# Attention with the values' projection last, and weight splits that wait for GpSimd's sum

## The reference, cut to what matters

```python
h = rmsnorm(x, norm_mix_2[i])          # x * rsqrt(mean(x*x) + eps) * gain
x = x + mixer(h)
x = x + (silu(rmsnorm(x, norm_ffn_2[i]) @ wg) * (rmsnorm(x, norm_ffn_2[i]) @ wu)) @ wd
```

```python
q, k, v = split(h @ w_qkv, [1024, 1280])
q, k = rmsnorm(q per head, q_gain), rmsnorm(k per head, k_gain)
logits = q @ k.T / 8 + bias, masked to a distance of at most 128
m = max(logits, sink); pr = exp(logits - m)
pr = pr / (sum(pr) + exp(sink - m))
out = (pr @ v) @ w_o
```

## Time and profile before

| | |
|---|---|
| median of 3 runs | 2970.85 us (2970.27 to 2976.11) |
| profiled execution | 2971.51 us, span 2969.6 us |
| mean granted clock of PE | 0.991 |
| PE busy | 2897.0 us, 98% |
| DVE, ACT, POOL busy | 2037.6, 1627.0, 330.4 us |
| DMA | 613.26 MB, mean 207 GB/s |
| attention, first projection to output projection | 2051.5 to 2147.1 us |

### The profile page before, as it was taken

The page is one execution under the profiler, slowest core; times in us unless marked ns, Lnnn a source line. Parts: engine busy times, 40 slices in busy tenths (PEclk is TensorE's granted clock), DMA queues, the critical chain, the costliest instruction groups (busy, mean ns, idle before and its releaser), DMA issues.

```text
span 2969.6 us, 46613 instructions
## 1 busy us (share of the span) xinstructions
PE 2897.0 (98%) x20144; PEld 2679.1 (90%) x20144; DVE 2037.6 (69%) x1842; ACT 1627.0 (55%) x1603; POOL 330.4 (11%) x224
## 2 busy tenths in 40 slices
PE   8999999999999999999999999999899999999999
PEld 8999999999988888888888787999799999896999
DVE  6787665678768888888888765555555555575553
ACT  6456544545657767767677552445654454362542
POOL 1130310113010000000000002101021111002210
PEclk9999999999999999999999999999999999999999
DMA  7444555544549989989899531556155545540453
GB/s 235 155 142 157 172 185 173 184 145 145 165 181 372 347 346 373 351 335 355 344 370 370 166 128 43 171 177 234 44 170 181 188 150 184 192 142 29 154 180 122
DMA packets 359730, 613.26 MB, mean 207 GB/s; under 512 B 11519, under 2 KB 323925, under 8 KB 324576
## 3 DMA queue, kind: packets, MB, share of 16 engines
q1 hardware_dynamic: 355936, 597.99, 57.8%
q10 hardware_dynamic: 3104, 12.10, 1.2%
q0 software_dynamic: 480, 0.12, 0.0%
HBM read 608.99 MB, written 1.05 MB: 205 GB/s over the span
## 4 chain that ended last, share of the span: by engine, by line
PE 94%; DVE 2%; ACT 2%; POOL 1%; issue 1%; DMA 0%; ACTq 0%; SPq 0%; POOLq 0%; DVEq 0%
PE ps L329 19%; PE ps L330 18%; PE ps L331 18%; PE ps L1269 5%; PE ps L1271 5%; PE ps L1270 5%; PE ps L1245 3%; PE ps L1247 3%; PE ps L1246 3%; PE ps L1810 2%; PE ps L689 2%; PE ps L1825 2%; PE ps L1319 1%; PE ps L1778 1%; PE ps L1766 1%; POOL work L392 1%
## 5 line engine op out<-in xcount | busy, mean ns | idle before, releaser
L273 DVE TENSOR_TENSOR wlo<-raw,whi 128x2048 fp32r<-128x2048 f32 (+2 forms) x574 | 1320.4, 2305 | 445.9 <-ACT whi L262 441.5
L262 ACT ACTIVATE whi<-raw 128x2048 fp32r<-128x2048 f32 (+2 forms) x574 | 1084.5, 1891 | 259.7 <-PE ps L331 134.9
L329 PE MATMUL ps<-HX,whi 128*128 128x256 f32 x1808 | 522.5, 289 | 16.5 <-DVE wlo L273 11.7
L330 PE MATMUL ps<-HX,whi 128*128 128x256 f32 x1808 | 513.9, 284 | 0.0
L331 PE MATMUL ps<-HX,wlo 128*128 128x256 f32 x1808 | 513.8, 284 | 0.0
L329 PE MATMUL ps<-HXB,whi 128*128 128x256 f32 x1760 | 503.0, 286 | 2.7 <-DVE HXB L448 2.7
L330 PE MATMUL ps<-HXB,whi 128*128 128x256 f32 x1760 | 499.7, 284 | 0.0
L331 PE MATMUL ps<-HXB,wlo 128*128 128x256 f32 x1760 | 499.4, 284 | 0.0
L329 PEld LDWEIGHTS ps<-HX,whi 128*128 128x128 f32 x1808 | 349.2, 193 | 22.8 <-ACT HX L524 10.4
L330 PEld LDWEIGHTS ps<-HX,whi 128*128 128x128 f32 x1808 | 349.4, 193 | 3.2 <-issue 3.1
L331 PEld LDWEIGHTS ps<-HX,wlo 128*128 128x128 f32 x1808 | 349.2, 193 | 0.0
(11 more groups left out here) (337 smaller groups left out, 4276.0 us busy)
## 6 DMA issues: line engine op xcount, KB each, us to landing
raw<-in_c_experts SPq DMA_DIRECT2D x264, 1024.0 KB, 4.9
raw<-in_w_in SPq DMA_DIRECT2D x71, 1024.0 KB, 5.0
raw<-in_ff_w_gate SPq DMA_DIRECT2D x44, 1024.0 KB, 5.4
raw<-in_ff_w_up SPq DMA_DIRECT2D x44, 1024.0 KB, 5.3
raw<-in_ff_w_down SPq DMA_DIRECT2D x32, 1024.0 KB, 5.3
raw<-in_dense_w SPq DMA_DIRECT2D x30, 1024.0 KB, 5.3
raw<-in_hy_w_in SPq DMA_DIRECT2D x24, 1024.0 KB, 5.2
raw<-in_ff_w_down SPq DMA_DIRECT2D x16, 768.0 KB, 4.6
```

The source lines that it names most:

```text
L262: e.activation(m.whi[:, i % NSPLIT, 0:n], m.raw[:, i % NRAW, 0:n], ACT.Copy).then_inc(*k.up("act", "hi", i))
L273: e.tensor_tensor(m.wlo[:, i % NRAW, 0:n], m.raw[:, i % NRAW, 0:n], hi, ALU.subtract).then_inc(*k.up("dve", "lo", i))
L329: e.matmul(o, wh, xh, start=first and t == k0, stop=False)
L330: e.matmul(o, wh, xl, start=False, stop=False)
```

## The change

1. In `dve_out`, `dve_ffn` (where another stage's input is prepared) and `dve_hyena`, DVE waits for "sq sum" in front of the last `dve_panel` call of the stage.
2. In attention the panels come as k, q0 to q3, v, and the three engines' orders follow. PE: k, sum, q0, head norm 0, q1, head norm 1, keys doubled, q2, head norm 2, scores 0, head norm 3, q3, scores 1, turned 0, head norm 4, factors, scores 2, v, scores 3, turned 1, values 0, values 1, turned 2, turned 3, back 0, values 2, values 3, back 1 to 3, output. `values_in` and `keys_doubled` are the loops of before as functions.

```diff
-    for part in (4, 0, 5, 1, 2, 3):
+    for part in (4, 0, 1, 2, 3, 5):
...
         if j == 3:
             dve_ahead(e, k, m, s, 6, 2, nxt)
+            e.wait_ge(*k.at("sq sum", s))
         dve_panel(e, k, m, panels)
...
         if j == 3:
             dve_ahead(e, k, m, s, 7, 1, nxt)
+            if nxt:
+                e.wait_ge(*k.at("sq sum", s))
         dve_panel(e, k, m, panels)
...
     pe_gemm(e, k, m, s, "q", m.HX, [0])
     headnorm(0)
+    pe_gemm(e, k, m, s, "q", m.HX, [1])
+    headnorm(1)
+    keys_doubled()
+    pe_gemm(e, k, m, s, "q", m.HX, [2])
+    headnorm(2)
+    scores(0)
+    headnorm(3)
+    pe_gemm(e, k, m, s, "q", m.HX, [3])
+    scores(1)
+    turned(0)
+    headnorm(4)
     pe_factors_down(e, k, m, s, last)
...
     scores(2)
+    values_in()
+    scores(3)
+    turned(1)
     values(0)
-    turned(1)
-    scores(3)
     values(1)
     turned(2)
+    turned(3)
+    back(0)
     values(2)
-    back(0)
-    turned(3)
-    back(1)
     values(3)
-    back(2)
-    back(3)
+    for g in (1, 2, 3):
+        back(g)
...
     act_panel(e, k, m, panels)
+    act_panel(e, k, m, panels)
     act_rstd(e, k, m, last, m.rs[:, :])
     squares(0, m.buf(1)[:, 0:512], "k", 0)
+    headnorm(0)
     query_squares(0)
-    headnorm(0)
     act_panel(e, k, m, panels)
+    query_squares(1)
+    headnorm(1)
+    keys_doubled()
+    act_panel(e, k, m, panels)
+    query_squares(2)
+    headnorm(2)
+    headnorm(3)
+    exps(0)
+    query_squares(3)
+    act_panel(e, k, m, panels)
+    turned(0)
+    headnorm(4)
     act_factors_down(e, k, m, s)
...
     exps(1)
-    headnorm(4)
-    turned(0)
+    values_in()
     exps(2)
     turned(1)
     exps(3)
     turned(2)
-    high(0)
     turned(3)
-    for g in (1, 2, 3):
+    act_panel(e, k, m, panels)
+    for g in range(4):
         high(g)
...
+    dve_panel(e, k, m, panels)
     queries(0)
     headnorm(0)
-    dve_panel(e, k, m, panels)
+    queries(1)
     headnorm(1)
-    queries(1)
+    queries(2)
     softmax(0)
     headnorm(2)
-    queries(2)
+    queries(3)
+    headnorm(3)
     softmax(1)
-    headnorm(3)
-    queries(3)
     turned(0)
+    dve_panel(e, k, m, panels)
     softmax(2)
     headnorm(4)
+    softmax(3)
+    turned(1)
+    dve_panel(e, k, m, panels)
     values(0)
-    turned(1)
-    softmax(3)
     values(1)
     turned(2)
+    turned(3)
     values(2)
     low(0)
-    turned(3)
-    low(1)
     values(3)
-    low(2)
-    low(3)
+    for g in (1, 2, 3):
+        low(g)
+    dve_panel(e, k, m, panels)
+    dve_panel(e, k, m, panels)
     dve_out(e, k, m, panels, s, nxt)
```

More of the change, by code:

```diff
@@ L2204, in back, with keys_doubled, values_in @@
         mm.then_inc(*k.up("mm", "ot", s, g))
+    def keys_doubled():
+        e.wait_ge(*k.at("normed", s, 0))
+        for j in range(2):
+            o = pe_take(e, k, m, "kd", s, j)
+            for i in range(2):
+                for half in range(2):
+                    mm = e.matmul(o[64 * half:64 * half + 64, i * L:(i + 1) * L], m.ident[:, 64 * i:64 * i + 64],
+                                  K[:, j * L:(j + 1) * L], start=True, stop=True)
+            mm.then_inc(*k.up("mm", "kd", s, j))
+    def values_in():
+        n = pe_panel(e, k, m)
+        wh, wl = weights(m, n, 8, 256)
+        o = pe_take(e, k, m, "v", s)
+        for j in range(2):
+            oj = o[:, j * 256:j * 256 + 256]
+            for t in range(8):
+                xh, xl = (m.HX[:, p, t, j * 128:j * 128 + 128] for p in range(2))
+                e.matmul(oj, xh, wh[:, t, :], start=t == 0, stop=False)
+                e.matmul(oj, xh, wl[:, t, :], start=False, stop=False)
+                mm = e.matmul(oj, xl, wh[:, t, :], start=False, stop=t == 7)
+        mm.then_inc(*k.up("mm", "v", s))
+        k.note("mm", "used", n)
     pe_gemm(e, k, m, s, "k", m.HX, [0], fresh=("hx", last))
@@ L2209, in pe_attn @@
     headnorm(0)
-    pe_factors_down(e, k, m, s, last)
[L2211 to L2235, removed]
-    headnorm(3)
-    scores(1)
-    pe_gemm(e, k, m, s, "q", m.HX, [3])
-    headnorm(4)
-    turned(0)
+    pe_gemm(e, k, m, s, "q", m.HX, [1])
[9 more added lines that the diff above has]
+    headnorm(4)
+    pe_factors_down(e, k, m, s, last)
     scores(2)
+    values_in()
+    scores(3)
+    turned(1)
     values(0)
-    turned(1)
-    scores(3)
     values(1)
     turned(2)
+    turned(3)
+    back(0)
     values(2)
-    back(0)
-    turned(3)
-    back(1)
     values(3)
-    back(2)
-    back(3)
+    for g in (1, 2, 3):
+        back(g)
     pe_gemm(e, k, m, s, "out", m.HX, range(4), fresh=("ax", s))
@@ L2279, in query_squares, with keys_doubled, values_in @@
     def query_squares(j):
-        act_panel(e, k, m, panels)
         squares(1 + j, m.buf(0)[:, 512 * j:512 * j + 512], "q", j)
+    def keys_doubled():
+        for j in range(2):
+            e.wait_ge(*k.at("kd", s, j))
+            e.activation(m.buf(1)[:, 1024 + 512 * j:1536 + 512 * j], ps(k, m, "kd", s, j)[:, :], ACT.Copy).then_inc(
+                *k.up("act", "free", "kd", s, j))
+    def values_in():
+        e.wait_ge(*k.own("act"))
+        e.wait_ge(*k.at("v", s))
+        for j in range(2):
+            vs = slice(256 * j, 256 * j + 256)
+            e.activation(m.buf(2)[:, vs], ps(k, m, "v", s)[:, vs], ACT.Copy, scale=m.rst[:, j:j + 1]).then_inc(*k.up("act", "free", "v", s))
     def exps(g):
@@ L2305, in act_attn @@
     act_panel(e, k, m, panels)
+    act_panel(e, k, m, panels)
     act_rstd(e, k, m, last, m.rs[:, :])
     squares(0, m.buf(1)[:, 0:512], "k", 0)
+    headnorm(0)
     query_squares(0)
-    headnorm(0)
     act_panel(e, k, m, panels)
-    act_factors_down(e, k, m, s)
[L2312 to L2327, removed]
+    query_squares(1)
[10 more added lines that the diff above has]
+    headnorm(4)
+    act_factors_down(e, k, m, s)
     exps(1)
-    headnorm(4)
-    turned(0)
+    values_in()
     exps(2)
```

## The result

The changed kernel takes 2932.02 us (median of 4 executions, 2930.85 to 2932.49), the kernel before 2973.48 with the runs made beside it added; the ratio is 0.986, with a 95% interval of 0.9843 to 0.9877. The forecast was 2932.0 in a range of 2925 to 2944. The profiled span fell from 2969.6 to 2930.2 us, by 39.4. The interval leaves out 1, so a gain of 1.4% is clear of the noise.

What follows compares the result with a forecast made beforehand. TensorE (PE), the chain ending last at 94% of the span, was taken as the bound; 23.1 us from the waits plus 16.0 from attention made 39.1, giving 2932 us, in a range of 2925 to 2944.

Steps and rivals of the forecast that it cites:

- What GpSimd waits for: Adds before the norm's sum: GpSimd stands still while DVE splits weights, so 1.30 us becomes 5.50 at attention's exit.
- Rival C: GpSimd's slowness is not DVE's doing: adds stay at 5.5 us, edges give nothing, total 2957 us; chance 0.03.
- Six terms of the sum: Passages between stages, norm's sum plus second panel: gains of three times 4.7, then 3.15, 2.2 and 3.6 us.
- the three put at 4.7: Edges from a mixer into an FFN, at 337, 1862 and 2176 us: 10.87 us each falls to 6.18.
- 3.15: Fourth edge into an FFN, equally long idle but with clock 1.00: 9.33 us falls to 6.18.
- 2.2: Edge into the second mixer: 8.41 us falls to 6.18.
- The term of 3.6 us: Into the pooling: PE's wait before the sum goes and the whole stretch of 15.69 us moves earlier by 3.6.
- 78.7 us: Attention in the new order: 73.3 us of PE work plus 5.4 idle, against 95.58, saving 16.9.
- the half drop: Attention, 2091 to 2100 us: half of a 1.8 us clock loss allowed for small waits, lowering the saving to 16.0.
- Rivals A and B: Attention: A, ACT and DVE set its pace, 2940 us, chance 0.17; B, only the entry's 2.5 gained, 2945, chance 0.07.
- Rival E: Attention: PE stays at 1.2 GHz because new waits come too often; slower, 2992 us; chance 0.01.
- rival D: Whole kernel: 44 to 50 us gained as attention's waits and drops vanish, 2924 us; chance 0.07.

Runs made afterwards that it cites:

- the second execution: The changed kernel run again, unaltered, beside the kernel with filled pooling and both attention splits moved: median 2933.48 us.
- the filled one: Changed kernel plus matmuls whose results nobody reads, in PE's idle time in the pooling and the next FFN's first panel: 2932.10 us, ratio 0.9853.
- Two edits of 1.2 and 2.9 us: Against the changed kernel: ACT's second attention split moved behind k's squares (2937.20 us); unread matmuls filling PE's idle time around the pooling (2932.10 us).

## Why the prediction was right

**What GpSimd waits for.** Right, and now shown and not only read from the rows: 3.33 us beside two SBUF inputs, 1.31 beside one. The free adds are 1.30 and 0.74 us, the prices of the earlier trace rows. Rival C falls with it. The picture was half of it, though: GpSimd does not always stand still. Of two instructions side by side the one that started first goes on, and behind the pooling that is twice GpSimd's add, at DVE's cost.

**The edges.** Six terms of the sum were edges. Five of them came out as priced: 4.57, 4.67, 4.69 for the three put at 4.7, 3.14 for 3.15, 2.23 for 2.2. PE does not wait for L380 any more, and the wait costs DVE nothing that anyone misses, with a cover measured at 5.2 us at the first mixer's exit and over 4.4 at attention's. The clock's share in these terms is luck in part. The kernel with the new order and without the waits has the same idle of 2.91 to 2.93 us at the four edges into an FFN, and its clock fell at two of them (341.4 and 1870.6), where the kernel before has three.

**The pooling.** The term of 3.6 us measured 0.83 in the changed kernel's profile. The chain did move as foreseen: the windows' first matmul starts 4.83 us behind the end of the panel in front of the sum, where it was 8.47 before, so it moved by 3.64. The matmuls from there on then ran partly at 1.2 GHz, in two stretches of 3.4 us, one at 2339.8 and one at 2353.4. The kernel before had one, at 2374.0, but ahead of the windows, where PE waits anyway; from the windows' first matmul to the end of the next first panel it took 16.12 us, and the changed kernel 18.93 with two drops. I had left the clock out of this one term, while I had it in all others. In the second execution there was no drop, that part took 16.14 us, and 20.97 against 24.59 is 3.6. So the mechanism was right and the size holds for the execution without drops; with one drop it is 1.9 to 2.2, and that was the commonest case in the profiles.

**Attention.** 78.7 us were worked out before the half drop, 77.96 measured; 16.9 saved, 17.6 measured. PE busy is 74.18 for 73.3, idle 3.8 for 5.4. Of the 17.6, 9.5 us are idle of PE that is gone (13.3 before), and 8.1 are busy time (82.28 before) in which matmuls had run at half clock. The waits stand where the queues put them, with 1.1, 0.8, 0.6 and 2.1 us from start to start for 1.3, 1.5, 0.6 and 1.9; turning 0 is the one that was sized too long. The 0.9 us that I took off for the clock was too careful for the profiled executions of this kernel, but two of the kernels with the same order (the filled one and the one with ACT's split later) lost 1.5 us to it. Rivals A and B fall: ACT's 61.4 us of work did not set the pace, and its head norms went under the panels. Rival E falls with the clock of 1.00.

**The sum.** 39.1 forecast and 39.4 measured between the spans. That it fits to 0.3 us is partly chance: the pooling gave 2.8 less, attention 1.6 more, and 1.7 came from stages without an edit. That the time forecast, 2932, was met is luck on top: it was worked out from the first median of 2970.85, which with the run made beside the change became 2973.48, so that the medians lie 41.5 us apart. It is still short of rival D's 44. What a forecast of this kernel can claim is some 4 us, since the experts' stage alone differs by that between two executions of the changed kernel.

## What to carry to other kernels

Before an engine's slow instruction is made faster, look at what its neighbour does in the same microseconds: an add of 1.3 us took 5.5 because another engine had begun to prepare something not due for 5 us. Ordering such work behind the urgent one is free as long as the cover is counted in the consumer's panels. And where PE must wait in small pieces, put the stretches that only feed other engines (projections, here) between a result and its use, in the order in which the slower engines need them; price the clock wherever PE still waits, as a bound on both sides and not as a certain gain or loss.

## What the runs showed of the hardware

- A DVE instruction with two SBUF inputs that started first holds up a GpSimd add for as long as it runs (3.33 us); a reduction with one input of the same length does not (1.31 us), nor do DVE instructions with one input in SBUF, one in PSUM and a full output in SBUF (1.27 us). An add that started first holds up such a DVE instruction in turn (1.19 us instead of 0.69).
- The same program had, between the same two matmuls, 23.76 us with the clock at 0.86 in one execution and 20.97 with the clock at 1.00 in another, with the same waits of PE in between (0.9 to 1.5 us of idle each). Behind such waits the clock fell in some executions, and five us of idle in 21 went without a drop in others.
- A drop of 3.4 us that begins during or behind a wait cost 1.5 us of panel work (attention of 79.5 us and not 78.0; an edge of 10.87 and not 9.33), which is as much as many a reordering gains. Two edits of 1.2 and 2.9 us could be seen in their stretch and not in the time of the whole.
